# Feed-forward hidden rows: transposed by VectorE in 32x32 squares and sixteen small DMAs, in place of TensorE

## The chip, the cores and the metric

The kernel runs on one core of a Trainium2 chip. TensorE multiplies, VectorE (DVE in the rows) and ScalarE (ACT) do elementwise work, GpSimd (POOL) does a few small steps, and SyncE (SP) issues DMAs. All weights come from the chip's main memory (HBM) in every execution. The metric is the device time of one execution in microseconds (us), the median of several.

## What is computed

Two blocks of two layers each, on 256 tokens of width 1024 in float32. Each layer has two feed-forward stages, a mixer between them and a gated embedding at the end; so there are eight feed-forward stages. Only these are touched:

```python
def swiglu_2(x, wi, wo):
    gate, up = jnp.split(x @ wi, 2, axis=-1)
    return (jax.nn.silu(gate) * up) @ wo

# in every layer, twice (the first block alike, with its own weights):
h = h + 0.5 * rms_norm_2(swiglu_2(rms_norm_2(h, g[0]), ffn_wi_2[i, 0], ffn_wo_2[i, 0]), g[1])
...
h = h + 0.5 * rms_norm_2(swiglu_2(rms_norm_2(h, g[4]), ffn_wi_2[i, 1], ffn_wo_2[i, 1]), g[5])
```

The hidden width is 2816. `x @ wi` gives 2 x 2816 columns, and the product of the gated half with the other half is the left operand of `@ wo`.

## The kernel before, in words

**Matmuls.** A float32 weight is split into a high part (`wh`, written by ScalarE, L634) and a low part (`wl`, the difference, written by VectorE, L820), and so is each left operand (`XH`, `XL`; `AH`, `AL` for the hidden rows). Each product is three matmuls of 128x128 by 128x512: high by high (L516), high by low (L517), low by high (L518).

**Weights.** They come in chunks of mostly 1 MB into three buffers (`raw`), and SP issues the loads in the order of the chunks (`load`, L1109 and L1111: in the up layer of a feed-forward stage two DMAs of 512 KB for a chunk, in the out layer one DMA). A load waits until the chunk three places ahead of it has been split. A chunk has two parts of two rows of tiles each. A part is split into one of seven `wh`/`wl` buffers, so ScalarE rounds part j + 7 (`round`) when TensorE has used part j, and VectorE makes the low part behind it (`leave`). A part is four steps of three matmuls, two steps for each of the two row tiles (t = 0, 1).

**A feed-forward stage.** The up layer has 11 blocks of 512 columns (256 gate columns, 256 up columns), each of 4 parts, so 44 parts in 22 chunks. When both row tiles of block b are done, ScalarE writes tanh of the gate half to a buffer `att` (one of three, L764) and VectorE makes the gated rows of it in four instructions (L966 and L969 for t = 0 and t = 1). These rows have the tokens on the partitions, and the out layer wants them the other way round. So TensorE transposes them, four 128x128 tiles a block, through the identity into a PSUM bank (`pe_turn_hidden`, L542), at a fixed step (12 steps behind the block's last for most blocks; a block has 16). Then ScalarE copies the bank to `AH` (`act_hidden`, L734), and VectorE writes the difference to `AL` (`dve_hidden`, L939). The out layer (22 parts in 12 chunks, two blocks of columns over 22 rows of tiles) reads `AH` and `AL` of hidden block b in its part b.

**Order.** Each engine runs its list in the order in which the code is written: `during` puts extra TensorE work at numbered steps, and the loops over `layer.parts` in `act_ffn`, `dve_ffn`, `act_out` and `dve_out` place the rest at numbered parts. No scheduler moves anything. Engines wait for each other by counting semaphores (`wait_ge`).

Of the kernel before, what the change touches and what calls it, by code (L numbers as in the profile page):

```python
# [14 lines left out]
P = 128  # L15
# [238 lines left out]
class Net:  # L254


    def __init__(self, nc, A, out, ctx, stages):
# [53 lines left out]
        self.AL = at("AL", EO + FF // P * S * 4, [P, FF // P, S], F32R)  # L311

# [113 lines left out]
        self.hid_hi, self.hid_lo = count("hid_hi"), count("hid_lo")  # L426

# [108 lines left out]
    def pe_turn_hidden(self, pe, n, b):  # L536
        bank = self.turn_bank(pe, ("hid", n, b), (self.hid_hi, n, b), (self.hid_lo, n, b))
        hid = self.att[b % 3]
        for i in range(2):
            for t in range(T):  # L540
                pe.wait_ge(self.gated, n, b, t)
                m = pe.e.transpose(bank[:, i * S + t * P:i * S + (t + 1) * P],  # L542
                                   hid[:, t * FB + i * P:t * FB + (i + 1) * P], self.ident[:, :])
        m.then_inc(*self.turned.up("hid", n, b))

# [129 lines left out]
    def act_out(self, act, n):  # L675
# [67 lines left out]
    def act_ffn(self, act, n):  # L743
        layer = self.layers[n, "up"]
        sc = self.cols(2 * T, "sc", n)
        for i, p in enumerate(layer.parts):
# [5 lines left out]
            if i == 7:  # L752
                self.act_hidden(act, n, 0)
            elif i >= 10 and i % 4 == 2:
                self.act_hidden(act, n, i // 4 - 1)
            self.round(act, p.j + N_W)
            if i % 4 == 3:
                b = i // 4
                for t in range(T):
                    act.wait_ge(self.used[t], layer.end[b])  # L760
                    act.wait_ge(self.sc, n, "all")
                    if b >= 3:
                        act.wait_ge(self.turned, "hid", n, b - 3)
                    act.e.activation(self.att[b % 3][:, t * FB:(t + 1) * FB], self.pair((n, "up", b))[t][:, 0:FB],  # L764
                                     ACT.Tanh, scale=sc[:, t:t + 1]).then_inc(*self.tanh.up(n, b, t))
# [129 lines left out]
    def dve_out(self, dve, n):  # L895
# [3 lines left out]
        for i, p in enumerate(layer.parts):  # L899
            if STAGES[n][0] == "ffn" and i == 2:  # L900
                self.dve_hidden(dve, n, NFB - 1)
# [46 lines left out]
    def dve_ffn(self, dve, n):  # L948
        layer = self.layers[n, "up"]
        sc = self.cols(2 * T, "sc", n)  # L950
        for i, p in enumerate(layer.parts):
# [3 lines left out]
            if i == 7:  # L955
                self.dve_hidden(dve, n, 0)
            elif i >= 10 and i % 4 == 2:
                self.dve_hidden(dve, n, i // 4 - 1)
# [12 lines left out]
        self.dve_out(dve, n)
# [140 lines left out]

    def sync(self, e, final):
# [9 lines left out]
        for c in range(self.all_chunks):  # L1123
# [1919 lines left out]
```

## Time and profile before

| | |
|---|---|
| median of 3 runs | 2273.22 us (2271.8 to 2273.25) |
| the profiled execution, its span | 2272.0 us |
| TensorE busy, share of the span | 2238.2 us, 99% |
| VectorE busy | 1467.2 us, 65% |
| ScalarE busy | 1155.1 us, 51% |
| DMA: bytes, mean rate | 395.61 MB, 174 GB/s |
| SP's DMA queue (q1), share of 16 DMA engines | 50.1% |
| granted TensorE clock | 0.998 of full speed, which is 2.4 GHz |

Busy times of matmuls overlap, since one starts before the one ahead of it has ended, so a TensorE at 99% is not at its peak rate. What a step costs is read from the distance between starts, or from the chain of waits: that is the chain of work that ended last, followed back from the end, each piece with the time it adds. Idle time of an engine off that chain costs nothing by itself.

### The profile page before, as it was taken

The page shows a single profiled execution, that of the slowest core. Times are in us where ns is not written, and L with a number is a line of the kernel's source. Part 1 is how long each engine was busy: PE and PEld are TensorE (multiplying, and loading weights), DVE is VectorE, ACT ScalarE, POOL GpSimd, SP SyncE. Part 2 cuts the span into 40 slices and gives each one's busy share as a digit, 9 for nine tenths or more (in the row PEclk, how much of TensorE's full clock was granted, in tenths as well). Part 3 has the DMA queues.
Part 4 walks back from the last instruction along what each step waited for, and adds up shares of the span by engine and source line. Part 5 has one row for each costly group of instructions (what it writes and reads, how often), then busy time and mean ns, then how long its engine had stood idle before and what let it go on. Part 6 is the DMA issues. An engine that isn't in the chain of part 4 may idle for free.

```text
span 2272.0 us, 33788 instructions
## 1 busy us (share of the span) xinstructions
PE 2238.2 (99%) x13383; PEld 1820.8 (80%) x13383; DVE 1467.2 (65%) x2079; ACT 1155.1 (51%) x1668; POOL 180.8 (8%) x286
## 2 busy tenths in 40 slices
PE   8999999999999999999999999999999999999998
PEld 6888888888888768878887888877888788868887
DVE  6655756656765877676567656656656765677655
ACT  5445545445544454354455445455445544565444
POOL 1001001001000010420011001001001100051001
PEclk9999999999999999999999999999999999999999
DMA  7555655555655640065556555534555555526553
GB/s 254 186 185 198 226 177 192 185 186 176 207 188 189 202 160 12 8 222 183 186 179 196 185 186 197 187 94 153 185 188 189 190 185 185 196 76 199 185 177 111
DMA packets 290091, 395.61 MB, mean 174 GB/s; under 512 B 11752, under 2 KB 193328, under 8 KB 289936
## 3 DMA queue, kind: packets, MB, share of 16 engines
q1 hardware_dynamic: 285072, 377.20, 50.1%
q0 software_dynamic: 4720, 16.20, 2.0%
q8 instruction: 108, 1.77, 0.3%
q14 instruction: 47, 0.39, 0.1%
q10 hardware_dynamic: 144, 0.07, 0.0%
HBM read 392.37 MB, written 1.05 MB: 173 GB/s over the span
## 4 chain that ended last, share of the span: by engine, by line
PE 94%; DVE 3%; ACT 1%; issue 1%; POOL 0%; DMA 0%; DVEq 0%; SPq 0%; POOLq 0%; ACTq 0%
PE bank L516 28%; PE bank L518 27%; PE bank L517 27%; PE bank L542 2%; PE bank L530 1%; PE bank L2560 0%; PE bank L1449 0%; PE bank L2554 0%; ACT wh L634 0%; ACT JUNK L641 0%; PE bank L2571 0%; PE bank L1964 0%; PE bank L1186 0%; DVE H L887 0%; DVE qPS L1902 0%
## 5 line engine op out<-in xcount | busy, mean ns | idle before, releaser
L820 DVE TENSOR_TENSOR wl<-raw,wh 128x1024 fp32r<-128x1024 f32 x708 | 859.1, 1223 | 556.5 <-ACT wh L634 556.2
L634 ACT ACTIVATE wh<-raw 128x1024 fp32r<-128x1024 f32 x708 | 744.4, 1058 | 650.9 <-PE bank L518 626.1
L516 PE MATMUL bank<-wh,XH 128*128 128x512 f32 x2000 | 801.7, 401 | 7.0 <-DVE wl L820 5.7
L518 PE MATMUL bank<-wh,XL 128*128 128x512 f32 x2000 | 781.7, 391 | 0.0
L517 PE MATMUL bank<-wl,XH 128*128 128x512 f32 x2000 | 781.5, 391 | 0.0
L516 PEld LDWEIGHTS bank<-wh,XH 128*128 128x128 f32 x2000 | 376.6, 188 | 96.8 <-issue 17.5
L518 PEld LDWEIGHTS bank<-wh,XL 128*128 128x128 f32 x2000 | 376.4, 188 | 81.6
L517 PEld LDWEIGHTS bank<-wl,XH 128*128 128x128 f32 x2000 | 377.2, 189 | 72.6 <-issue 0.5
L516 PE MATMUL bank<-wh,AH 128*128 128x512 f32 x704 | 276.0, 392 | 0.0
L518 PE MATMUL bank<-wh,AL 128*128 128x512 f32 x704 | 274.1, 389 | 0.0
L517 PE MATMUL bank<-wl,AH 128*128 128x512 f32 x704 | 274.1, 389 | 0.0
L518 PEld LDWEIGHTS bank<-wh,AL 128*128 128x128 f32 x704 | 132.2, 188 | 27.5
L517 PEld LDWEIGHTS bank<-wl,AH 128*128 128x128 f32 x704 | 132.2, 188 | 26.8
L516 PEld LDWEIGHTS bank<-wh,AH 128*128 128x128 f32 x704 | 132.2, 188 | 26.9
L1036 POOL TENSOR_SCALAR ST<-ST 128x1 f32<-128x1 f32 x32 | 9.2, 287 | 1358.0 <-ACT JUNK L641 1357.8
L734 ACT ACTIVATE AH<-bank 128x512 fp32r<-128x512 f32 x88 | 52.7, 599 | 113.9 <-PE bank L542 113.9
L939 DVE TENSOR_TENSOR AL<-bank,AH 128x512 fp32r<-128x512 f32 x88 | 60.8, 691 | 57.6 <-ACT AH L734 57.6
L969 DVE SCALAR_TENSOR_TENSOR att<-att,ST,bank 128x256 f32<-128x256 f32 x176 | 84.6, 481 | 6.2
L764 ACT ACTIVATE att<-bank,ST 128x256 f32<-128x256 f32 x176 | 72.3, 462 | 12.7 <-POOL ST L1076 12.7
L966 DVE SCALAR_TENSOR_TENSOR att<-att,bank 128x256 f32<-128x256 f32 x176 | 72.8, 414 | 5.2 <-ACT att L764 5.2
L646 ACT ACTIVATE XH<-CT 128x512 fp32r<-128x512 f32 x60 | 37.2, 628 | 76.6 <-DVE CT L837 71.9
L641 ACT ACTIVATE JUNK<-bank 128x512 bf16<-128x512 f32 x48 | 28.4, 591 | 55.3 <-PE bank L518 55.2
(339 smaller groups left out, 1722.5 us busy)
## 6 DMA issues: line engine op xcount, KB each, us to landing
raw<-in_ffn_w_dram SPq DMA_DIRECT2D x182, 512.0 KB, 4.6
raw<-in_ffn_wi_dram SPq DMA_DIRECT2D x176, 512.0 KB, 4.7
raw<-in_ffn_w_dram SPq DMA_DIRECT2D x40, 1024.0 KB, 4.9
raw<-in_ffn_wo_dram SPq DMA_DIRECT2D x40, 1024.0 KB, 4.8
raw<-in_a_wqkv_dram SPq DMA_DIRECT2D x18, 1024.0 KB, 4.8
raw<-in_a_w_in_dram SPq DMA_DIRECT2D x16, 1024.0 KB, 5.1
raw<-in_b_w_in_dram SPq DMA_DIRECT2D x12, 1024.0 KB, 4.9
bc<-in_norm_g_dram POOLq DMA_DIRECT2D x16, 512.0 KB, 5.2
```

The source lines that it names most:

```text
L516: pe.e.matmul(o, a, h, start=(k == 0), stop=False)
L517: pe.e.matmul(o, a, l, start=False, stop=False)
L518: m = pe.e.matmul(o, b, h, start=False, stop=(k == layer.nk - 1))
L542: m = pe.e.transpose(bank[:, i * S + t * P:i * S + (t + 1) * P], hid[:, t * FB + i * P:t * FB + (i + 1) * P], self.ident[:, :])
L634: act.e.activation(self.wh[j % N_W][:, 0:p.size], self.raw[p.chunk % N_RAW][:, p.at:p.at + p.size], ACT.Copy).then_inc(*self.rounded.up(j))
L646: act.e.activation(self.XH[:, 4 * b:4 * b + 4, t * P:(t + 1) * P], self.CT[b][:, :, :], ACT.Copy).then_inc(*self.x_hi.up(n, t, b))
L734: act.e.activation(self.AH[:, 2 * b:2 * b + 2, :], bank.rearrange("p (k s) -> p k s", k=2), ACT.Copy).then_inc(*self.hid_hi.up(n, b))
L764: act.e.activation(self.att[b % 3][:, t * FB:(t + 1) * FB], self.pair((n, "up", b))[t][:, 0:FB], ACT.Tanh, scale=sc[:, t:t + 1]).then_inc( ...
L820: dve.e.tensor_tensor(self.wl[j % N_W][:, 0:p.size], self.raw[p.chunk % N_RAW][:, p.at:p.at + p.size], self.wh[j % N_W][:, 0:p.size].bitca ...
L939: dve.e.tensor_tensor(lo, bank.rearrange("p (k s) -> p k s", k=2), hi.bitcast(F32), ALU.subtract).then_inc(*self.hid_lo.up(n, b))
L966: dve.e.scalar_tensor_tensor(x, x, 1.0, pair[:, 0:FB], ALU.add, ALU.mult).then_inc(*self.gate.up(n, b, t))
L969: dve.e.scalar_tensor_tensor(x, x, sc[:, T + t:T + t + 1], pair[:, FB:2 * FB], ALU.mult, ALU.mult).then_inc(*self.gated.up(n, b, t))
```

## The change

In each of the eight feed-forward stages, and for each of the 11 hidden blocks:

- `pe_turn_hidden`, its four TensorE transposes and its PSUM bank are gone.
- ScalarE's tanh and VectorE's gating write the `att` buffer with columns in another order (same sizes, the two halves k ahead of the row tiles t), and VectorE transposes the whole buffer in place, 32x32 square by square, right behind the gating (`dve_turn_squares`).
- SP moves the squares to their places in a new float32 tile `AF` with 16 DMAs, each of 32 partitions x 4 runs of 32 floats (128 bytes a run, 16 KB a DMA): eight behind the load of the chunk that is the up layer's chunk 2b + 9, and eight behind the next chunk's load (`sp_hidden`). For b from 7 on these loads belong to the out layer.
- `AF` lies over `AL` (the same bytes); ScalarE copies `AF` to `AH` and VectorE writes `AF` minus `AH` to `AL`. ScalarE waits for the block's 16 DMAs (`d_hid`) where it waited for TensorE.
- Both steps stand later in the order: for block b at part 4b + 12 of the up layer's loop, right behind the tanh (VectorE: the gating) of block b + 2, in place of part 4b + 6 (part 7 for block 0). Blocks 8, 9 and 10 stand at parts 0, 4 and 8 of the out layer's loop, in place of parts 38 and 42 of the up layer's and part 2 of the out layer's.
- ScalarE's tanh of block b + 3 waits for the DMAs of block b, in place of its TensorE transposes.

The diff, cut:

```diff
+        self.AF = at("AF", EO + FF // P * S * 4, [P, FF // P, S], F32)
...
+    def hidden(self, b, t):
+        return self.att[b % 3][:, :].rearrange("p (k t c) -> p k t c", k=2, t=T)[:, :, t, :]
...
-    def pe_turn_hidden(self, pe, n, b):
-        bank = self.turn_bank(pe, ("hid", n, b), (self.hid_hi, n, b), (self.hid_lo, n, b))
...
-            if STAGES[n][0] == "ffn" and i == 2:
-                self.act_hidden(act, n, NFB - 1)
+            if STAGES[n][0] == "ffn" and i in (0, 4, 8):
+                self.act_hidden(act, n, NFB - 3 + i // 4)
...
     def act_hidden(self, act, n, b):
-        bank = self.bank(self.place["turn", ("hid", n, b)])
-        act.wait_ge(self.turned, "hid", n, b)
-        act.e.activation(self.AH[:, 2 * b:2 * b + 2, :], bank.rearrange("p (k s) -> p k s", k=2), ACT.Copy).then_inc(
+        act.wait_ge(self.d_hid[b % 3], n, b, 3, 3)
+        act.e.activation(self.AH[:, 2 * b:2 * b + 2, :], self.AF[:, 2 * b:2 * b + 2, :], ACT.Copy).then_inc(
             *self.hid_hi.up(n, b))
...
-            if i == 7:
-                self.act_hidden(act, n, 0)
-            elif i >= 10 and i % 4 == 2:
-                self.act_hidden(act, n, i // 4 - 1)
+            if i >= 12 and i % 4 == 0:
+                self.act_hidden(act, n, i // 4 - 3)
...
+    def dve_turn_squares(self, dve, n, b):
+
+        hid = self.att[b % 3]
+        dve.wait_ge(self.gated, n, b, 1)
+        dve.e.transpose(hid[:, :], hid[:, :]).then_inc(*self.squares_turned.up(n, b))
...
+    def sp_hidden(self, sp, n, b, half):
+
+        hid = self.att[b % 3][:, :].rearrange("p (k j c) -> p k j c", k=2 * T, j=4)
+        whole = self.AF[:, 2 * b:2 * b + 2, :].rearrange("p k (t i c) -> p (k t) i c", t=T, i=4)
+        sp.wait_ge(self.squares_turned, n, b)
+        for i in (2 * half, 2 * half + 1):
+            for j in range(4):
+                sp.e.dma_start(whole[32 * j:32 * j + 32, :, i, :], hid[32 * i:32 * i + 32, :, j, :]).then_inc(
+                    *self.d_hid[b % 3].up(n, b, i, j, by=16))
...
+            for n in range(self.n_stages):
+                if STAGES[n][0] == "ffn":
+                    block, half = divmod(c - self.layers[n, "up"].parts[0].chunk - 9, 2)
+                    if 0 <= block < NFB:
+                        self.sp_hidden(sp, n, block, half)
```

SP's list in the first up layer, before, where the loads of chunks 9 and 10 stand (`raw` is the weight buffer; a load names the semaphores for which it waits):

```order
L1109 DMA raw_54<-in_ffn_w_dram 128x4x256 [waits left,rounded]
L1111 DMA raw_54<-in_ffn_w_dram 128x4x256
L1109 DMA raw_55<-in_ffn_w_dram 128x4x256 [waits left,rounded]
L1111 DMA raw_55<-in_ffn_w_dram 128x4x256
L1109 DMA raw_56<-in_ffn_w_dram 128x4x256 [waits left,rounded]
L1111 DMA raw_56<-in_ffn_w_dram 128x4x256
```

and the same place now:

```order
L1100 DMA raw_54<-in_ffn_w_dram 128x4x256 [waits left,rounded]
L1102 DMA raw_54<-in_ffn_w_dram 128x4x256
L1111 DMA AF<-att_78 32x4x32 [waits squares_turned]
L1111 DMA AF<-att_78 32x4x32 x7
L1100 DMA raw_55<-in_ffn_w_dram 128x4x256 [waits left,rounded]
L1102 DMA raw_55<-in_ffn_w_dram 128x4x256
L1111 DMA AF<-att_78 32x4x32 x8
```

Behind every load of the stretch stand eight small DMAs, and the next load stands behind them.

VectorE's list at the end of an up block, before (`wl` the low part of a weight, `att` the gated rows):

```order
L820 TENSOR_TENSOR wl_68<-raw_54,wh_61 128x1024 [waits d_raw0,rounded]
L966 SCALAR_TENSOR_TENSOR att_80<-att_80,bank 128x256 [waits tanh]
L969 SCALAR_TENSOR_TENSOR att_80<-att_80,ST,bank 128x256 [waits gate]
L966 SCALAR_TENSOR_TENSOR att_80<-att_80,bank 128x256 [waits tanh]
L969 SCALAR_TENSOR_TENSOR att_80<-att_80,ST,bank 128x256 [waits gate]
L820 TENSOR_TENSOR wl_69<-raw_54,wh_62 128x1024 [waits rounded]
L820 TENSOR_TENSOR wl_70<-raw_55,wh_63 128x1024 [waits d_raw1,rounded]
L939 TENSOR_TENSOR AL<-bank,AH 128x512 [waits hid_hi]
```

and now:

```order
L808 TENSOR_TENSOR wl_68<-raw_54,wh_61 128x1024 [waits d_raw0,rounded]
L956 SCALAR_TENSOR_TENSOR att_80<-att_80,bank 128x2x128 [waits tanh]
L959 SCALAR_TENSOR_TENSOR att_80<-att_80,ST,bank 128x2x128 [waits gate]
L956 SCALAR_TENSOR_TENSOR att_80<-att_80,bank 128x2x128 [waits tanh]
L959 SCALAR_TENSOR_TENSOR att_80<-att_80,ST,bank 128x2x128 [waits gate]
L932 STREAM_TRANSPOSE att_80<-att_80 128x512 [waits gated]
L926 TENSOR_TENSOR AL<-AF,AH 128x512 [waits hid_hi]
L808 TENSOR_TENSOR wl_69<-raw_54,wh_62 128x1024 [waits rounded]
L808 TENSOR_TENSOR wl_70<-raw_55,wh_63 128x1024 [waits d_raw1,rounded]
```

The transpose and the write of `AL` now stand ahead of the low part of the weights for which SP's next load waits.

ScalarE's list at the same place, before:

```order
L764 ACTIVATE att_80<-bank,ST 128x256 [waits used0]
L764 ACTIVATE att_80<-bank,ST 128x256
L634 ACTIVATE wh_62<-raw_54 128x1024 [waits used1]
L634 ACTIVATE wh_63<-raw_55 128x1024 [waits used1,d_raw1]
L734 ACTIVATE AH<-bank 128x512 [waits turned]
```

and now:

```order
L751 ACTIVATE att_80<-bank,ST 128x2x128 [waits used0]
L751 ACTIVATE att_80<-bank,ST 128x2x128
L723 ACTIVATE AH<-AF 128x512 [waits d_hid0]
L624 ACTIVATE wh_62<-raw_54 128x1024 [waits used1]
L624 ACTIVATE wh_63<-raw_55 128x1024 [waits used1,d_raw1]
```

The copy to `AH` now waits for DMAs and stands ahead of the rounding of the next weights.

## Rows read from the trace of the kernel before

**Rows 1.** The page: busy time by engine, and the chain's shares by engine.

```profile
PE 2238.2 (99%) x13383; PEld 1820.8 (80%) x13383; DVE 1467.2 (65%) x2079; ACT 1155.1 (51%) x1668; POOL 180.8 (8%) x286
...
PE 94%; DVE 3%; ACT 1%; issue 1%; POOL 0%; DMA 0%; DVEq 0%; SPq 0%; POOLq 0%; ACTq 0%
```

**Rows 2.** Waits over the span: who for whom, us in total, times, longest.

```profile
ACT wh L634 <- PE bank L518: 626.1, 458, 5.5
...
ACT wh L634 <- DMA raw<-in_ffn_w_dram: 5.9, 5, 2.8
```

**Rows 3.** The chain in order of time, one up block: start us, us, what.

```profile
600.05 0.23 PE bank L518
600.27 0.44 PE bank L542 x4
600.71 0.24 PE bank L516
...
604.17 0.23 PE bank L516
...
611.66 0.44 PE bank L542 x4
```

**Rows 4.** One block's window: us, each engine's busy us, clock, DMA share, GB/s.

```profile
609.49:620.86 11.37, 11.37 (x54) 9.40 (x53) 7.12 (x9) 5.57 (x7) 0.00 (x0) 1.00 0.61 185
```

**Rows 5.** The page's costliest groups: count, busy us, mean ns, idle before.

```profile
L820 DVE TENSOR_TENSOR wl<-raw,wh 128x1024 fp32r<-128x1024 f32 x708 | 859.1, 1223 | 556.5 <-ACT wh L634 556.2
L634 ACT ACTIVATE wh<-raw 128x1024 fp32r<-128x1024 f32 x708 | 744.4, 1058 | 650.9 <-PE bank L518 626.1
...
L734 ACT ACTIVATE AH<-bank 128x512 fp32r<-128x512 f32 x88 | 52.7, 599 | 113.9 <-PE bank L542 113.9
...
L969 DVE SCALAR_TENSOR_TENSOR att<-att,ST,bank 128x256 f32<-128x256 f32 x176 | 84.6, 481 | 6.2
...
L646 ACT ACTIVATE XH<-CT 128x512 fp32r<-128x512 f32 x60 | 37.2, 628 | 76.6 <-DVE CT L837 71.9
```

**Rows 6.** Groups between 300 and 400 us, a VectorE subtraction from SBUF.

```profile
L843 DVE TENSOR_TENSOR XL<-CT,XH 128x512 fp32r<-128x512 f32 x4 | 2.7, 687 | 0.5 <-ACT XH L646 0.4
```

**Rows 7.** ScalarE in time at a block's end: start, us, instruction, idle before.

```profile
605.24 0.82 ACT L764 ACTIVATE att<-bank,ST 128x256 f32<-128x256 f32 x2
606.93 1.06 ACT L634 ACTIVATE wh<-raw 128x1024 fp32r<-128x1024 f32 x1 [0.88 <-PE bank L518]
```

**Rows 8.** VectorE in time at the same block's end.

```profile
607.80 0.48 DVE L969 SCALAR_TENSOR_TENSOR att<-att,ST,bank 128x256 f32<-128x256 f32 x1
608.20 1.22 DVE L820 TENSOR_TENSOR wl<-raw,wh 128x1024 fp32r<-128x1024 f32 x1
```

**Rows 9.** SP's DMA issues in time: start us, us that the issue took.

```profile
1.64 1.98 SPq L1105 DMA_DIRECT2D raw<-in_ffn_w_dram  x4
...
4.73 0.80 SPq L1118 DMA_DIRECT2D H<-in_x_dram  x1
...
609.49 0.37 SPq L1109 DMA_DIRECT2D raw<-in_ffn_w_dram  x1
609.91 0.50 SPq L1111 DMA_DIRECT2D raw<-in_ffn_w_dram  x1
...
756.93 0.96 SPq L2375 DMA_DIRECT2D rW<-in_b_a_dram  x1
```

**Rows 10.** DMA issues over the span: count, KB each, us from issue to landing.

```profile
raw<-in_ffn_w_dram SPq DMA_DIRECT2D x182, 512.0 KB, 4.6
...
out_dram<-H SPq DMA_DIRECT2D x4, 256.0 KB, 2.1
```

**Rows 11.** SP's queue, 600 to 660 us: packets, MB, share of 16 DMA engines.

```profile
q1 hardware_dynamic: 11472, 11.39, 59.5%
```

**Rows 12.** The same, 757 to 760 us, with the sizes of its packets.

```profile
DMA packets 1910, 0.87 MB, mean 290 GB/s; under 512 B 968, under 2 KB 1903, under 8 KB 1910
...
q1 hardware_dynamic: 1910, 0.87, 102.4%
```

More of the change, by code:

```diff
@@ L426, in __init__ @@
         self.hid_hi, self.hid_lo = count("hid_hi"), count("hid_lo")
+        self.squares_turned = count("squares_turned")
+        self.d_hid = [count(f"d_hid{i}") for i in range(3)]
         self.weighed, self.msum, self.rstd, self.resid = (count(x) for x in ("weighed", "msum", "rstd", "resid"))
@@ L534, in x_ready @@
         return lambda k, t: [(self.x_hi, n, t, k // 4), (self.x_lo, n, t, k // 4)]
-    def pe_turn_hidden(self, pe, n, b):
-        bank = self.turn_bank(pe, ("hid", n, b), (self.hid_hi, n, b), (self.hid_lo, n, b))
[L538 to L544, printed above, removed]
     def pe_turn_next(self, pe, n, name, step):
@@ L762, in act_ffn @@
                     if b >= 3:
-                        act.wait_ge(self.turned, "hid", n, b - 3)
-                    act.e.activation(self.att[b % 3][:, t * FB:(t + 1) * FB], self.pair((n, "up", b))[t][:, 0:FB],
+                        act.wait_ge(self.d_hid[b % 3], n, b - 3, 3, 3)
+                    act.e.activation(self.hidden(b, t), self.pair((n, "up", b))[t][:, 0:FB].rearrange(
+                        "p (k c) -> p k c", k=2),
                                      ACT.Tanh, scale=sc[:, t:t + 1]).then_inc(*self.tanh.up(n, b, t))
@@ L899, in dve_out @@
         for i, p in enumerate(layer.parts):
-            if STAGES[n][0] == "ffn" and i == 2:
-                self.dve_hidden(dve, n, NFB - 1)
+            if STAGES[n][0] == "ffn" and i in (0, 4, 8):
+                self.dve_hidden(dve, n, NFB - 3 + i // 4)
             if i == half - 1:
@@ L935, in dve_hidden @@
     def dve_hidden(self, dve, n, b):
-        bank = self.bank(self.place["turn", ("hid", n, b)])
-        hi, lo = (x[:, 2 * b:2 * b + 2, :] for x in (self.AH, self.AL))
+        hi, lo, whole = (x[:, 2 * b:2 * b + 2, :] for x in (self.AH, self.AL, self.AF))
         dve.wait_ge(self.hid_hi, n, b)
-        dve.e.tensor_tensor(lo, bank.rearrange("p (k s) -> p k s", k=2), hi.bitcast(F32), ALU.subtract).then_inc(
-            *self.hid_lo.up(n, b))
+        dve.e.tensor_tensor(lo, whole, hi.bitcast(F32), ALU.subtract).then_inc(*self.hid_lo.up(n, b))
+    def dve_turn_squares(self, dve, n, b):
+        hid = self.att[b % 3]
+        dve.wait_ge(self.gated, n, b, 1)
+        dve.e.transpose(hid[:, :], hid[:, :]).then_inc(*self.squares_turned.up(n, b))
     def dve_p(self, dve, n):
@@ L954, in dve_ffn @@
                 self.dve_p(dve, n)
[L955 to L958, printed above, removed]
+            if i >= 12 and i % 4 == 0:
+                self.dve_hidden(dve, n, i // 4 - 3)
             self.leave(dve, p.j + N_W)
@@ L962, in dve_ffn @@
                 for t in range(T):
-                    x = self.att[b % 3][:, t * FB:(t + 1) * FB]
-                    pair = self.pair((n, "up", b))[t]
+                    x = self.hidden(b, t)
+                    pair = self.pair((n, "up", b))[t].rearrange("p (s k c) -> p s k c", s=2, k=2)
                     dve.wait_ge(self.tanh, n, b, t)
-                    dve.e.scalar_tensor_tensor(x, x, 1.0, pair[:, 0:FB], ALU.add, ALU.mult).then_inc(
+                    dve.e.scalar_tensor_tensor(x, x, 1.0, pair[:, 0], ALU.add, ALU.mult).then_inc(
                         *self.gate.up(n, b, t))
                     dve.wait_ge(self.gate, n, b, t)
-                    dve.e.scalar_tensor_tensor(x, x, sc[:, T + t:T + t + 1], pair[:, FB:2 * FB], ALU.mult,
+                    dve.e.scalar_tensor_tensor(x, x, sc[:, T + t:T + t + 1], pair[:, 1], ALU.mult,
                                                ALU.mult).then_inc(*self.gated.up(n, b, t))
+                self.dve_turn_squares(dve, n, b)
         self.dve_out(dve, n)
```

6 lines of the change are left out of this document (removed).

## The prediction, written before the changed kernel ran

> **What bounds the kernel now.** I read the page first. TensorE is busy 99% of the span and has 94% of the chain that ended last; VectorE is at 65% and ScalarE at 51% [rows 1]. The waits say who follows whom: ScalarE's rounding of weights waits for TensorE 626.1 us in 458 waits, and for a weight DMA 5.9 us in 5 [rows 2]. So the weight pipeline runs ahead, held back by TensorE, and what TensorE no longer does should come off the end. The chain in order of time then prices the transposes [rows 3]: from 600.27 to 611.66 us one block of an up layer passes, 11.39 us. The four transposes are one piece of 0.44 us. From 604.17 to 611.66 stand 33 matmuls, 7.49 us or 0.227 each. From 600.71 to 604.17 stand 15, 3.46 us or 0.231 each: behind the transposes the matmuls are a little slow, 0.06 us in all. In a window of one block VectorE is busy 7.12 us and ScalarE 5.57 of 11.37, the DMA engines 61% [rows 4]. In this stretch there is room everywhere but on TensorE.
>
> **What is removed.** 88 groups of four transposes: the hidden copy to AH has the count, 88 [rows 5]. Each is 0.44 us of the chain, 38.7 us; with all of the slow matmuls behind them it would be 0.50, 44 us. The matmul right behind has 0.24 us for 0.227 [rows 3], so 0.01 at least belongs to the switch: I take 0.45, and 88 x 0.45 = **39.6 us**. A block then takes 10.9 us, a chunk of weights 5.46, a part 2.73.
>
> **What is added on VectorE.** 88 transposes of 128x512 in place. No row shows one. Nearest by size: a VectorE subtraction of 128x512 from SBUF takes 687 ns [rows 6]; the bounds are 481 ns for 128x256 and 1223 ns for 128x1024 [rows 5]. I take 0.69 us. A block costs VectorE 7.12 + 0.69 = 7.8 of 10.9 us, 8.4 at the upper bound. It fits, price nothing as long as the delay doesn't reach TensorE (below). AH is now copied from SBUF, 628 ns by the row of XH, for 599 [rows 5], also hidden. The reordered columns change no size; I price them at nothing.
>
> The Trainium skill ("VectorE: DVE Perf Modes", The three transpose paths) lists TensorE at 390 ns and VectorE at 311 ns for 128x128 in bf16, the latter in 32x32 blocks only. No row here has a VectorE transpose; the sum would be the same by it, since VectorE is not the bound.
>
> **What is added on SP.** 1408 DMAs of 16 KB, eight behind the load of each chunk in 22 of a stage's 34 chunks. SP's own time is the first thing that can run out. Issued alone, a DMA takes 0.37 us, the second of a pair 0.50, and the pair 0.92 from start to end [rows 9]. Four in a row took 1.98 us, 0.50 each [rows 9]. So load and eight small ones are 0.92 + 8 x 0.50 = 4.9 us of a period of 5.46. It fits, but SP goes from idle to 90% full. Bounds per small DMA: 0.37, and 0.96 for one behind others of many short runs [rows 9]; 0.80 was also seen near the start. I take 0.50: these have 128 runs each, fewer than the 256 of the four.
>
> **What is added on the DMA engines.** 1024 packets of 128 bytes a chunk. Between 600 and 660 us a packet (nearly all 1 KB) took 0.595 x 60 x 16 / 11472 = 50 ns [rows 11], so a chunk's load is 1024 x 50 / 16 = 3.2 us of each engine. Between 757 and 760 us, with half of the packets under 512 bytes, the mean was 1.024 x 3 x 16 / 1910 = 26 ns [rows 12]. Bounds for 128 bytes: near zero, and 50. I take 26 as an upper guess: 1024 x 26 / 16 = 1.7 us, 4.9 in all of 5.46. Even at 50 it would be 6.4, and that falls behind by 0.9 us a chunk, 21 us in a stage, about as much as the lead computed below.
>
> **The waits, and the lead.** The second half of block b's DMAs stands behind a load that waits for VectorE's low part; that stands behind VectorE's transpose and AL write, and the AL write waits for ScalarE's AH copy, which waits for the DMAs of the block before. This is a loop, once a block. Before, the low part ran from 608.20 to 609.42 and SP started at 609.49 [rows 8, 9]; now 0.69 + 0.69 us stand ahead of it, so SP starts 1.4 us later. From SP's start: 0.92 + 8 x 0.50 + 2.1 for landing (a small store lands in 2.1, a weight load in 4.6 [rows 10]) = 7.0 us; AH 0.63; rounding 1.06; low part 1.22; hand-offs 0.3: 10.2 us against a block of 10.9. The loop closes in time. In place: a block ends near 604.2, ScalarE comes to the AH copy at 606.06, behind the tanh [rows 7]; the squares have landed at 609.49 - 10.9 + 1.4 + 7.0 = 607.0. So ScalarE waits about 0.9 us a block, and the next rounding, due at 606.93 [rows 7], starts near 607.6. Queued behind that wait are the next weights, and nobody is late: they are for seven parts on, TensorE holds six full ones, 6 x 2.73 = 16.4 us, less the 2.4 us of making one, so a lead of 14 us. In the out layer, block 10 is copied at part 8 and needed at part 10, about 3 us of cover after its 0.63 + 0.69. SP's wait on the squares costs nothing: they are done at 609, and the load that precedes the first half waits for later work. The raw buffers add some 4 us of lead on SP's side: a load is issued about two chunks ahead, 10.9 us, and lands in 4.6, less the 1.4 of the delay. Price of the whole: nothing.
>
> **Sum.** 2272.0 - 39.6 = 2232.4 for the profiled execution; the median lies 1.2 above its span, so **2233.6 us**. Own range, with 0.44 to 0.50 a group: 2229 to 2235.
>
> **Rivals.**
>
> *Stalls at the edges.* The loop keeps time within a stage, but where the up layer ends and where block 10 is needed the lead is short, or the later low part holds the first weights of the next stage. For it: the delay of 1.4 us is on the path by which weights come. Against: only 5.9 us of DMA waits before. At 1 to 3 us a stage, 8 to 24 us of 40 go: 2242 to 2258.
>
> *SP's queue becomes the pace (slower).* Place: SP, up layers. Per chunk SP needs 0.92 + 8x against 5.46. The lag over 22 chunks, less the lead of 14 + 4 = 18 us, reaches TensorE: it decides from x = 0.67 us. At 0.85 (the row of 0.80 and a gap of 0.05): 7.7 us a chunk, 2.26 x 22 - 18 = 31.7 us a stage, 254 in eight, so 2233.6 + 254 = 2487; at 0.96 + 0.04: 8.9 us, 465 us more, near 2700. For it: rows of 0.80 and 0.96. Against: those stood behind DMAs of far more bytes or runs.
>
> *The DMA engines become the pace (slower).* Writes so short may cost more than their bytes. At twice the 50 ns packet: 3.2 + 6.4 = 9.6 us a chunk, (4.1 x 22 - 18) x 8 = 580 us more. It decides from 3.2 + 0.064p = 6.28, p = 48 ns. Against: the 26 ns mean of a mixed stretch. The Trainium skill ("DMA: Bandwidth & Descriptors", Specifications) says that below 512 B the engines read, modify and write, and its rules say to coalesce small transfers; the same page (Why small descriptors are slow) says that moves within SBUF escape the penalty. No row here is a move within SBUF, so both stand.
>
> *No change.* TensorE's list is shorter but something as slow stands behind it, so the 40 us come back as waits: 2269 to 2278. Against: 458 waits of ScalarE for TensorE.
>
> **How the numbers follow.** Chances: hidden 0.64, edges 0.15, no change 0.04, SP 0.10, DMA engines 0.07. The first two are faster by over 0.2% (4.5 us, about what a measurement of this kernel can tell): 0.79; same 0.04; slower 0.17. The range 2227 to 2262 holds the first two, 0.79; its low end leaves 2 us for a larger share of the slow matmuls.
>
> **What would show it.** Right: no L542 in the chain, an up block of 10.9 us, small DMAs issued at 0.50 us or less, ScalarE's AH copy waiting about 1 us for DMAs, rounding still waiting for TensorE. Wrong: matmuls waiting for `wl` or `wh` in the up layers, SP issues of over 0.67 us, a DMA share near 100% there, a weight landing time well over 4.6 us; or AH copies of block 10 that TensorE waits for. A VectorE transpose of over 10.9 - 7.1 = 3.8 us would make VectorE the bound.

## The result, and the profile after

The changed kernel takes 2382.35 us in the median of 4 runs (2379.46 to 2384.24), before 2273.23 us; the ratio is 1.0478, with a 95% interval of 1.0465 to 1.0491. It is 109 us slower, where 40 us faster was foretold.

The page of the changed kernel, first busy time by engine, then the chain that ended last by engine and by line (L1111 is the issue of a square's DMA, L522 to L524 are the three matmuls):

```profile
PE 2242.6 (94%) x13031; PEld 1809.4 (76%) x13031; DVE 1520.8 (64%) x2167; ACT 1129.8 (47%) x1668; POOL 183.6 (8%) x286
...
PE 50%; SPq 26%; DMA 9%; ACT 5%; DVE 4%; issue 4%; POOL 1%; DVEq 0%; POOLq 0%; ACTq 0%
SPq L1111 23%; PE bank L522 14%; PE bank L523 14%; PE bank L524 14%; ACT wh L624 3%; DMA raw<-in_ffn_w_dram 3%; DMA raw<-in_ffn_wi_dram 3%; SPq L1102 2%; SPq L1100 2%; DMA AF<-att 1%; DMA raw<-in_ffn_wo_dram 1%; DVE wl L808 1%; PE bank L536 1%; ACT JUNK L631 1%; PE bank L2566 0%
```

In [rows 1] TensorE had 94% of the chain and SP nothing. Now TensorE has 50% and SP's queue 26%, nearly all of it the squares' issues. SP's issues in time, in an up layer and in an out layer (start us, us, what, how many in a row):

```profile
622.25 0.37 SPq L1100 DMA_DIRECT2D raw<-in_ffn_w_dram  x1
622.67 0.50 SPq L1102 DMA_DIRECT2D raw<-in_ffn_w_dram  x1
623.22 5.10 SPq L1111 DMA_DIRECT2D AF<-att  x8
628.42 0.54 SPq L1100 DMA_DIRECT2D raw<-in_ffn_w_dram  x1
629.01 0.51 SPq L1102 DMA_DIRECT2D raw<-in_ffn_w_dram  x1
629.56 5.10 SPq L1111 DMA_DIRECT2D AF<-att  x8
634.75 0.54 SPq L1100 DMA_DIRECT2D raw<-in_ffn_w_dram  x1
...
1402.89 0.54 SPq L1102 DMA_DIRECT2D raw<-in_ffn_wo_dram  x1
1403.47 5.09 SPq L1111 DMA_DIRECT2D AF<-att  x8
1408.66 0.54 SPq L1102 DMA_DIRECT2D raw<-in_ffn_wo_dram  x1
```

Eight small DMAs take 5.10 us, 0.64 each with the gap between them, and the next load stands right behind: SP has no idle time left. A chunk takes it 634.75 - 628.42 = 6.33 us in the up layer, where TensorE needs a chunk every 5.46, and 5.77 us in the out layer. The page's groups for the copies, the matmuls on AH and VectorE's transpose, and the landing of the small DMAs:

```profile
L522 PE MATMUL bank<-wh,AH 128*128 128x512 f32 x704 | 293.4, 417 | 97.1 <-DVE AL L926 80.0
L723 ACT ACTIVATE AH<-AF 128x512 fp32r<-128x512 f32 x88 | 55.6, 632 | 494.0 <-DMA AF<-att 494.0
...
L926 DVE TENSOR_TENSOR AL<-AF,AH 128x512 fp32r<-128x512 f32 x88 | 60.9, 692 | 312.4 <-ACT AH L723 312.1
...
L932 DVE STREAM_TRANSPOSE att<-att 128x512 f32<-128x512 f32 x88 | 62.6, 712 | 3.0
...
AF<-att SPq DMA_DIRECT2D x1408, 16.0 KB, 2.9
```

ScalarE waits for squares before every one of the 88 copies, 494 us in all or 5.6 us each, where it waited 113.9 us for TensorE [rows 5]. TensorE waits on the hidden rows (97 us at L522, most of it for AL).

Where it waits is plain from the layers. From an up layer's first matmul to the out layer's first, and from there to the out layer's last, the sixth feed-forward stage took 127.6 and 61.0 us before; the changed kernel's takes 123.6 and 78.5. Over the eight stages the out layers went from 60.1 to 61.0 up to 75.7 to 80.1 us, 17 us each, and the up layers got 0.5 to 4.5 us shorter, 26 us in all. 8 x 17 = 136 us, less these 26, is the result.

Two of these stalls, in the fifth stage. ScalarE in time (start us, us, instruction, idle before and what ended it):

```profile
1415.59 0.63 ACT L723 ACTIVATE AH<-AF 128x512 fp32r<-128x512 f32 x1 [6.74 <-DMA AF<-att]
1416.12 1.04 ACT L624 ACTIVATE wh<-raw 128x1024 fp32r<-128x1024 f32 x1
1419.83 2.00 ACT L624 ACTIVATE wh<-raw 128x1024 fp32r<-128x1024 f32 x2 [2.67 <-DMA raw<-in_ffn_wo_dram]
1425.69 1.06 ACT L624 ACTIVATE wh<-raw 128x1024 fp32r<-128x1024 f32 x1 [3.86 <-DMA raw<-in_ffn_wo_dram]
1427.17 0.63 ACT L723 ACTIVATE AH<-AF 128x512 fp32r<-128x512 f32 x1 [0.42 <-DMA AF<-att]
```

VectorE's low parts of blocks 9 and 10:

```profile
1416.25 0.69 DVE L926 TENSOR_TENSOR AL<-AF,AH 128x512 fp32r<-128x512 f32 x1 [5.58 <-ACT AH L723]
...
1427.92 0.68 DVE L926 TENSOR_TENSOR AL<-AF,AH 128x512 fp32r<-128x512 f32 x1
```

TensorE there: the first matmuls of parts 9 and 10, with the idle time before them, and that of part 11:

```profile
1417.09 0.77 PE L522 MATMUL bank<-wh,AH 128*128 128x512 f32 x1 [4.00 <-DVE AL L926]
1428.75 0.77 PE L522 MATMUL bank<-wh,AH 128*128 128x512 f32 x1 [6.35 <-ACT wh L624]
...
1433.24 0.39 PE L522 MATMUL bank<-wh,AH 128*128 128x512 f32 x1
```

and windows of 4 us (busy us and instructions of PE, PEld, DVE, ACT, POOL; granted clock; DMA share; GB/s):

```profile
1408.00:1412.00 4.00, 4.00 (x19) 3.28 (x18) 2.67 (x3) 0.84 (x1) 0.00 (x0) 1.00 0.53 146
1412.00:1416.00 4.00, 1.09 (x5) 0.56 (x3) 0.00 (x0) 0.41 (x1) 0.00 (x0) 0.91 0.36 38
1416.00:1420.00 4.00, 2.91 (x7) 2.36 (x8) 1.92 (x2) 1.33 (x3) 0.00 (x0) 0.50 0.87 280
...
1424.00:1428.00 4.00, 0.00 (x0) 0.00 (x0) 1.22 (x2) 1.88 (x3) 0.00 (x0) 0.69 0.55 131
1428.00:1432.00 4.00, 3.25 (x8) 2.60 (x9) 1.83 (x3) 1.53 (x2) 0.00 (x0) 0.50 1.04 393
```

The hidden rows of blocks 9 and 10 end the two stalls, the second behind weights that had come late too. The view puts the second wait down to a rounding of weights, but `AL` of block 10 was done at 1427.92 + 0.68 = 1428.60 us, and TensorE goes on 0.15 us behind it, as it did behind `AL` of block 9 (1416.94 and 1417.09).

After each of these waits TensorE has the lower clock, 0.50 of full. The first matmul takes 0.77 us for 0.39, and the twelve of part 10 take 1433.24 - 1428.75 = 4.49 us, where those of part 11 take 2.72. The mean granted clock of the span fell from 0.998 to 0.974. The eight out layers are 140 us longer than in the kernel without the DMAs (the first experiment below). 97 of these are the idle time before L522, so the low clock makes up about 43, an estimate by difference. About 18 of the 43 lie behind the last wait of a layer; what lies ahead of a wait only shortens that wait.

### The profile page after: what moved, and what is told of

The parts are those of the page before. It is cut to its first block, busy times and chain, and to the rows that moved or that the text cites. A ratio compares the mean times of both kernels' runs of the same rounds, so it can differ in the third digit from the quotient of the medians.

```text
span 2382.4 us, 34582 instructions
## 1 busy us (share of the span) xinstructions
PE 2242.6 (94%) x13031; PEld 1809.4 (76%) x13031; DVE 1520.8 (64%) x2167; ACT 1129.8 (47%) x1668; POOL 183.6 (8%) x286
## 2 busy tenths in 40 slices
DMA packets 492851, 418.81 MB, mean 176 GB/s; under 512 B 214504, under 2 KB 396080, under 8 KB 492688
## 4 chain that ended last, share of the span: by engine, by line
PE 50%; SPq 26%; DMA 9%; ACT 5%; DVE 4%; issue 4%; POOL 1%; DVEq 0%; POOLq 0%; ACTq 0%
SPq L1111 23%; PE bank L522 14%; PE bank L523 14%; PE bank L524 14%; ACT wh L624 3%; DMA raw<-in_ffn_w_dram 3%; DMA raw<-in_ffn_wi_dram 3%; SPq L1102 2%; SPq L1100 2%; DMA AF<-att 1%; DMA raw<-in_ffn_wo_dram 1%; DVE wl L808 1%; PE bank L536 1%; ACT JUNK L631 1%; PE bank L2566 0%
## 5 line engine op out<-in xcount | busy, mean ns | idle before, releaser
L808 DVE TENSOR_TENSOR wl<-raw,wh 128x1024 fp32r<-128x1024 f32 x708 | 843.7, 1221 | 358.8 <-ACT wh L624 358.3
L624 ACT ACTIVATE wh<-raw 128x1024 fp32r<-128x1024 f32 x708 | 725.3, 1052 | 406.2 <-PE bank L524 267.1
L522 PE MATMUL bank<-wh,XH 128*128 128x512 f32 x2000 | 794.8, 397 | 15.4 <-DVE wl L808 14.1
L524 PE MATMUL bank<-wh,XL 128*128 128x512 f32 x2000 | 781.3, 391 | 0.0
L522 PEld LDWEIGHTS bank<-wh,XH 128*128 128x128 f32 x2000 | 376.9, 188 | 111.1 <-issue 19.0
L524 PEld LDWEIGHTS bank<-wh,XL 128*128 128x128 f32 x2000 | 377.0, 188 | 80.2
L522 PE MATMUL bank<-wh,AH 128*128 128x512 f32 x704 | 293.4, 417 | 97.1 <-DVE AL L926 80.0
L723 ACT ACTIVATE AH<-AF 128x512 fp32r<-128x512 f32 x88 | 55.6, 632 | 494.0 <-DMA AF<-att 494.0
L523 PE MATMUL bank<-wl,AH 128*128 128x512 f32 x704 | 287.7, 409 | 0.0
L524 PE MATMUL bank<-wh,AL 128*128 128x512 f32 x704 | 286.6, 407 | 0.0
L926 DVE TENSOR_TENSOR AL<-AF,AH 128x512 fp32r<-128x512 f32 x88 | 60.9, 692 | 312.4 <-ACT AH L723 312.1
L522 PEld LDWEIGHTS bank<-wh,AH 128*128 128x128 f32 x704 | 140.6, 200 | 139.0 <-issue 93.8
L524 PEld LDWEIGHTS bank<-wh,AL 128*128 128x128 f32 x704 | 140.3, 199 | 31.4
L523 PEld LDWEIGHTS bank<-wl,AH 128*128 128x128 f32 x704 | 141.2, 201 | 28.8
L932 DVE STREAM_TRANSPOSE att<-att 128x512 f32<-128x512 f32 x88 | 62.6, 712 | 3.0
```

What stands on the lines that cost most here:

```text
L522: pe.e.matmul(o, a, h, start=(k == 0), stop=False)
L523: pe.e.matmul(o, a, l, start=False, stop=False)
L524: m = pe.e.matmul(o, b, h, start=False, stop=(k == layer.nk - 1))
L624: act.e.activation(self.wh[j % N_W][:, 0:p.size], self.raw[p.chunk % N_RAW][:, p.at:p.at + p.size], ACT.Copy).then_inc(*self.rounded.up(j))
L723: act.e.activation(self.AH[:, 2 * b:2 * b + 2, :], self.AF[:, 2 * b:2 * b + 2, :], ACT.Copy).then_inc(*self.hid_hi.up(n, b))
L808: dve.e.tensor_tensor(self.wl[j % N_W][:, 0:p.size], self.raw[p.chunk % N_RAW][:, p.at:p.at + p.size], self.wh[j % N_W][:, 0:p.size].bitca ...
```

## The experiments

Where one execution is named, the kernel was timed once. The kernel before took 2270.7 to 2276.2 us beside all of these runs.

**Without the DMAs.** ScalarE and VectorE read `att` itself:

```diff
-        act.wait_ge(self.d_hid[b % 3], n, b, 3, 3)
+        act.wait_ge(self.squares_turned, n, b)
...
-                        self.sp_hidden(sp, n, block, half)
```

> Left out: the sixteen DMAs. ScalarE and VectorE take AH and AL straight from the att buffer behind VectorE's transpose, so the hidden rows stand in the wrong places. Theory A (SP's issuing is the pace; VectorE's and TensorE's side of the change is as foretold): the whole gain shows, an up block of 10.9 us, 2228 to 2234 us. Theory B (the later places of the copies, or VectorE's transpose ahead of the weights' low part, cost the time): still well above 2273.

Measured: 2230.18 us in one execution, span 2228.4. The chain in order of time, in an up layer (start us, us, what):

```profile
599.95 0.23 PE bank L522
600.18 0.23 PE bank L523
600.41 0.23 PE bank L524
...
611.51 0.23 PE bank L522
```

From 599.95 to 611.51 stand 51 matmuls, 0.227 us each, with nothing between them. So the gain was there, 2272.3 to 2228.4 us for the spans, 44 us, or 0.50 a group: the upper end of the foretold price. VectorE's transpose and the later copies cost nothing. All of the loss is in the sixteen DMAs.

**Fewer DMAs for the same bytes.** Eight a block, runs of 256 bytes:

```diff
-            for j in range(4):
-                sp.e.dma_start(whole[32 * j:32 * j + 32, :, i, :], hid[32 * i:32 * i + 32, :, j, :]).then_inc(
+            for j in range(2):
+                q = 32 * ((i + 1) % 4)
+                sp.e.dma_start(whole[q:q + 32, :, 2 * j:2 * j + 2, :], hid[32 * i:32 * i + 32, :, 2 * j:2 * j + 2, :]).then_inc(
```

> Eight DMAs a block in place of sixteen, four behind a load, with the same bytes in all (32 partitions x 4 runs of 256 bytes; squares land in the wrong places). Theory A (SP's time): 1.1 + 4 x 0.64 = 3.7 us a chunk against 5.46, so SP has time to spare and the kernel takes 2230 to 2240 us. Theory D (the bytes, or the latency of a move behind a load, is the pace and not the number of issues): little better than 2382.

Measured: 2238.14 us in one execution. SP's issues there:

```profile
610.52 0.37 SPq L1100 DMA_DIRECT2D raw<-in_ffn_w_dram  x1
610.94 0.51 SPq L1102 DMA_DIRECT2D raw<-in_ffn_w_dram  x1
611.49 2.53 SPq L1112 DMA_DIRECT2D AF<-att  x4
614.48 0.37 SPq L1100 DMA_DIRECT2D raw<-in_ffn_w_dram  x1
```

The issues cost the same 0.64 us each, but now SP waits for the pipeline again, and the 144 us are gone. All eight feed-forward stages are as long as without the DMAs, to 0.5 us. The 8 us above that kernel lie in the mixer, where TensorE ran at clock 0.50 from 865 to 882 us in this execution and at 1.00 in the other. Theory A stands against theory D: the bytes are the same. The packets are half as many too, though; the next kernels keep the number of issues and change the rest.

**What makes an issue cost 0.64 us.** Three kernels change the DMA alone: 32 runs of 512 bytes; all 128 partitions without a shift; and a source in HBM.

```diff
+                sp.e.dma_start(whole[q:q + 32, j, :, :], hid[32 * i:32 * i + 32, j, :, :]).then_inc(
...
+                sp.e.dma_start(whole[:, j, i, :], hid[:, i, j, :]).then_inc(
...
+                sp.e.dma_start(whole[32 * j:32 * j + 32, :, i, :], self.A["c_ident"][32 * i:32 * i + 32, :].rearrange(
```

> Sixteen DMAs a block of the same 16 KB each, as 32 runs of 512 bytes in place of 128 runs of 128; squares land in the wrong places. Theory A1 (an issue costs SP 0.64 us whatever its runs): eight in a row still 5.1 us, 2382 us. Theory A2 (the issue's price grows with the number of runs): eight in a row under 4.2 us and 2235 to 2260 us. Theory C (the DMA engines are held up by 128-byte packets): packets a quarter, so the time falls as in A2, but the issues on SP stay at 0.64 us.

> Sixteen DMAs a block, each over all 128 partitions with one run of 128 bytes, no shift between partitions (squares land in the wrong places); bytes, runs and DMA count as in the changed kernel. Theory A1 (fixed price of an issue): eight in a row 5.1 us, 2382 us. Theory A3 (the price comes from 32 partitions x 4 runs, two levels of pattern): eight in a row about 4.0 us, the 0.50 of the weight loads, and 2233 to 2245 us.

> The sixteen DMAs of the changed kernel with the same shape and place, but read from HBM (a constant) in place of the squares, so the hidden rows are wrong. Tells what made an issue 0.64 us where four weight loads in a row took 0.50. Theory S (a source in SBUF makes the issue dear): eight in a row 4.0 us, 2235 to 2260 us. Theory R (any DMA in a long row of DMAs costs it): eight in a row 5.1 us, 2375 to 2390 us.

Measured, one execution each: 2358.69, 2369.87 and 2379.55 us. Eight in a row, in this order:

```profile
704.09 4.94 SPq L1112 DMA_DIRECT2D AF<-att  x8
```
```profile
703.02 5.02 SPq L1111 DMA_DIRECT2D AF<-att  x8
```
```profile
703.95 5.05 SPq L1111 DMA_DIRECT2D AF<-in_c_ident_dram  x8
```

It is 4.9 to 5.1 us whatever the runs, the partitions or the source; the first kernel has a quarter of the packets, and 128 us of its time above 2230 remain. So the price is one of an issue as such when many stand in a row, and the number of packets isn't the cause. The small differences fit as well: summed over the trace, the 1408 issues take 863.0 us in the changed kernel and 838.9, 850.8 and 860.5 in these three, which is 24.1, 12.2 and 2.5 less, and the medians are 23.7, 12.5 and 2.8 us less. Why four weight loads at the start of the kernel took 0.50 each [rows 9] and these take 0.64 stays open.

**Off SP.** Half of the squares, then all, through GpSimd's queue, behind `pool_gain`:

```diff
+        pool.wait_ge(self.squares_turned, n, b)
+        for i in range(4):
+            for j in js:
+                pool.e.dma_start(whole[32 * j:32 * j + 32, :, i, :], hid[32 * i:32 * i + 32, :, j, :]).then_inc(
+                    *self.d_hidp[b % 3].up(n, b, i, j, by=16))
```

> Squares of column groups 2 and 3 are moved by GpSimd's queue, eight DMAs a block, as soon as VectorE has turned them; groups 0 and 1 by SP, four behind a load. Theory A (SP's time is the pace): SP 1.1 + 4 x 0.64 = 3.7 of 5.46 us, GpSimd 8 x 0.6 = 4.8 of 10.9: 2230 to 2240 us, faster than both kernels. Theory D (bytes or packets on the DMA engines): 2380.

> All sixteen DMAs from GpSimd's queue behind the turning, none from SP. GpSimd's issues took 0.53 to 0.62 us before, 16 of them 8.5 to 9.9 of 10.9 us, landed about 17 us behind the block's end and asked for at 23.7. Theory A: 2230 to 2240 us. Rival: with short runs a GpSimd issue costs over 0.68 us, and then it is the pace in place of SP; at 0.8 it lags 1.9 us a block and the kernel is between 2240 and 2400.

Measured: half 2240.39 us (2230.86 to 2241.26), ratio to before 0.9844 (0.9823 to 0.9865); all 2232.84 us (2231.87 to 2239.3), ratio 0.983 (0.9812 to 0.9847). GpSimd's issues, one row of the second kernel's:

```profile
629.83 8.67 POOL L1124 DMA_DIRECT2D AF<-att  x16 [2.23 <-DVE att L933]
```

Sixteen take it 8.67 us of a block's 10.9, 0.54 each, and then it waits for the next squares. The same 1408 DMAs with the same bytes cost nothing when they don't stand ahead of the weight loads. By themselves these two runs don't clear the DMA engines. In the trace SP's squares are packets of 128 bytes, 180224 of them in the changed kernel, and GpSimd's are packets of 1 KB. So the second kernel has no packet of 128 bytes, and the first has half as many. The next kernel has all 180224 again.

**Fewer issues by way of HBM.** Four DMAs write a block's squares to a scratch in the layout of AF, one reads it back a chunk later:

```diff
+        if half == 0:
+            sp.wait_ge(self.squares_turned, n, b)
+            for i in range(4):
+                sp.e.dma_start(dr.rearrange("(j c) (k i p) -> i c k j p", j=4, k=4, i=4)[i], hid[32 * i:32 * i + 32, :, :, :]).then_inc(
+                    *self.d_square[b % 3].up(n, b, i, by=16))
+            return
+        sp.wait_ge(self.d_square[b % 3], n, b, 3)
+        sp.e.dma_start(self.AF[:, 2 * b:2 * b + 2, :], dr.rearrange("q (k s) -> q k s", k=2)).then_inc(
+            *self.d_hid[b % 3].up(n, b, by=16))
```

> The squares go through a scratch in HBM: four DMAs (32 partitions x 16 runs of 128 bytes) write them behind the first load, one DMA of 128 partitions x 2 KB reads them back behind the next. Five issues a block in place of sixteen. Theory A: SP 0.92 + 4 x 0.64 = 3.5 us and 0.92 + 0.5 = 1.4 us a chunk: never the pace; 2230 to 2240 us. Rival: the runs of 128 bytes cost more on their way to HBM, or the wait for the write (over 3 us) holds up the weight loads behind it on SP: 2245 to 2300.

Measured: 2228.55 us (2226.72 to 2237.71), ratio to before 0.981 (0.9788 to 0.9831): 1.9% less than the kernel before, and as fast as the kernel without the DMAs. SP and the waits for these rows:

```profile
1261.70 4.30 SPq L1113 DMA_DIRECT2D hid_squares<-att  x4
1267.67 0.37 SPq L1102 DMA_DIRECT2D raw<-in_ffn_wi_dram  x1
1268.08 0.51 SPq L1104 DMA_DIRECT2D raw<-in_ffn_wi_dram  x1
1268.63 0.50 SPq L1117 DMA_DIRECT2D AF<-hid_squares  x1
```
```profile
ACT AH L725 <- DMA AF<-hid_squares: 27.7, 24, 2.9
```

The writes are dearer than foretold: these four took 0.58, 1.45, 0.72 and 1.43 us, and the 88 rows of four 2.6 to 6.5 us, 4.2 in the median; but a block is 10.9 us long. ScalarE waits 27.7 us in all for them. The packets of the second GpSimd kernel and of this one:

```profile
DMA packets 335155, 418.81 MB, mean 188 GB/s; under 512 B 34280, under 2 KB 238384, under 8 KB 334992
```
```profile
DMA packets 488620, 441.76 MB, mean 199 GB/s; under 512 B 199016, under 2 KB 380592, under 8 KB 488464
```

The changed kernel has 214504 packets under 512 bytes. This one has nearly as many, more bytes, and loses nothing, and that rules out the DMA engines as the cause. They have little room left, though: from 600 to 660 us their share is 0.87, where it was 0.60 before.

**Which work the lag reaches TensorE by.** The first try left block 10 to TensorE, at its old step:

```diff
+            if step == 12:
+                self.pe_turn_hidden(pe, n, NFB - 1)
...
-                    if 0 <= block < NFB:
+                    if 0 <= block < NFB - 1:
```

> Block 10 of each stage goes over TensorE as before (copy still at part 8 of the out layer); blocks 0 to 9 as in the changed kernel. Theory A (SP falls behind by some 0.87 us a chunk and the lag comes out at the hidden block that the out layer needs first): SP has two of 22 slots less, 11.6 us, but block 9 is then the late one and is needed one part, 2.7 us, sooner: of the 17 us that an out layer is longer 8 to 10 stay, about 2310 us. Theory E (only block 10 is short of cover, the others aren't): the out layer is as short as before, about 2240 us.

Measured: 2353.2 us in one execution, above both. The out layers are 71.7 to 75.2 us. TensorE's waits (us in total, times, longest):

```profile
PE bank L547 <- DVE att L976: 46.5, 16, 7.1
PE bank L522 <- DVE AL L943: 26.5, 8, 4.4
```

Its transposes (L547) now wait for gated rows: ScalarE's tanh of block 10 was late. So not only the copies were late but ScalarE's whole list. I hadn't foreseen this wait.

**SP's lag with nobody waiting for the squares.** To the kernel without DMAs I added as many from a constant into scratch, at the same places in SP's list, in four of the eight stages:

```diff
+        sp.wait_ge(self.squares_turned, n, b)
+        for i in (2 * half, 2 * half + 1):
+            for j in range(4):
+                sp.e.dma_start(row[32 * j:32 * j + 32, :, i, :], self.ident[32 * i:32 * i + 32, :].rearrange(
+                    "p (k c) -> p k c", k=4)).then_inc(*self.d_hid[b % 3].up(n, b, i, j, by=16))
```

> The kernel without DMAs of squares (hidden rows taken straight from att, in the wrong places), plus SP's sixteen DMAs a block as fillers (identity into scratch), at the same places in SP's list, in the four second feed-forward stages alone. Nobody but the weight loads waits behind them. Theory G (the weights' lead of some 18 us takes up SP's lag of 17 to 21 us; the loss came from the hidden rows, which have about 4 us of cover): 2230 to 2245 us. Theory H (late weight loads alone make the loss, as much as in the changed kernel, 17 us a stage): 2230 + 4 x 17 = 2298 us.

Measured: 2312.48 us in one execution, 82 us over 2230. 75 of them lie in the four out layers with fillers, 17 to 21 each; the rest lies in the mixer behind the third stage. Theory G falls: late weight loads alone are enough. But its profile has the same place. In the second feed-forward stage TensorE, then ScalarE:

```profile
511.21 0.77 PE L523 MATMUL bank<-wh,AH 128*128 128x512 f32 x1 [16.56 <-DVE AL L927]
```
```profile
494.80 1.06 ACT L625 ACTIVATE wh<-raw 128x1024 fp32r<-128x1024 f32 x1 [4.63 <-DMA raw<-in_ffn_w_dram]
501.79 2.00 ACT L625 ACTIVATE wh<-raw 128x1024 fp32r<-128x1024 f32 x2 [5.94 <-DMA raw<-in_ffn_w_dram]
508.15 1.06 ACT L625 ACTIVATE wh<-raw 128x1024 fp32r<-128x1024 f32 x1 [4.36 <-DMA raw<-in_ffn_w_dram]
509.12 0.61 ACT L724 ACTIVATE AH<-att 128x512 fp32r<-128x512 f32 x1
```

TensorE waits 16.56 us for AL of block 10. The rows for it had long been in `att`; ScalarE's copy stood behind four roundings of weights that TensorE needs only several parts later, and these waited for late loads.

**The same, with the copies ahead.**

```diff
-            if STAGES[n][0] == "ffn" and i in (0, 4, 8):
-                self.act_hidden(act, n, NFB - 3 + i // 4)
+            if STAGES[n][0] == "ffn" and i < 3:
+                self.act_hidden(act, n, NFB - 3 + i)
```

> As the fillers kernel, but the AH and AL copies of blocks 8, 9 and 10 stand at parts 0, 1 and 2 of the out layer's loop on ScalarE and VectorE, in place of 0, 4 and 8; SP's list is the same. The fillers kernel lost 20 us in each of four stages with no squares to wait for. Theory J (ScalarE's list is in order, the copy of block 10 stood behind the rounding of weights that come off SP late, and it is needed two parts later; the weights themselves are needed seven parts later): with the copies ahead, the loss falls from 20 to under 5 us a stage, 2230 to 2250 us. Theory H (late weights reach TensorE by themselves): 2300 to 2315 us, as before the move.

Measured: 2268.93 us in one execution, 39 us over 2230, 9 to 11 a stage. The order of three copies was worth half of the loss. The other half is more than theory J had: here TensorE waits for weights (24.4 us for `wl` in 9 waits), so each theory holds for a part. This split is shown for the fillers alone. In the changed kernel the squares of block 10 are themselves issued behind SP's late loads, and no run tells how much of its loss comes by each way.

**How many slots it takes.** Blocks 0 to 4, then 0 to 7, by DMAs, the rest by TensorE; and the five-block kernel with ScalarE's and VectorE's copies four parts later:

```diff
+            if step >= 44 and (step - 44) % 16 == 0 and (step - 44) // 16 + 1 >= NDMA:
+                self.pe_turn_hidden(pe, n, (step - 44) // 16 + 1)
...
-                    if 0 <= block < NFB:
+                    if 0 <= block < NDMA:
```

> Blocks 0 to 4 of each stage go by squares and DMAs, blocks 5 to 10 by TensorE at their old steps (copies at the new parts). Theory A with a lead (SP falls behind by at most 10 slots x 0.87 = 9 us, less than the 14 us by which the weights run ahead, and catches up): no stall, 40 groups x 0.49 = 19.6 us less than before, 2253 us. Rival F (every slot costs TensorE its 0.87 us at once): 2253 + 10 x 0.87 x 8 = 2323 us.

> Blocks 0 to 7 by squares and DMAs, 8 to 10 by TensorE. Theory A with a lead: 16 slots, a lag of 13 to 14 us, just what the lead holds: 64 groups x 0.49 = 31 us less, 2242 us, or up to 5 us a stage more if block 10's transposes wait for rows that ScalarE has late: 2242 to 2282. Rival F: 2242 + 16 x 0.87 x 8 = 2353 us.

> As the kernel with five blocks by DMAs, but ScalarE and VectorE take these five blocks four parts later (part 4b + 16), so they don't wait for squares. The five-block kernel was 38 us over the 2253 foretold. Theory K (ScalarE's waits for squares made its tanh late, and TensorE's transposes of the later blocks waited for the gated rows): no such waits, 2253 to 2262 us. Theory L (SP's late weight loads make ScalarE late in any case): 2275 to 2292 us.

Measured, one execution each: 2291.96, 2309.51 and 2296.46 us. All out layers of the first kernel take 60.1 to 61.0 us, as before; the loss is in the up layers, where two stalls a stage, of 0.4 to 1.1 and of 1.6 to 3.1 us, stand at TensorE's transposes of blocks 6 and 7. Neither side of my expectation holds: there is some lead, since the five-block kernel is 31 us under rival F, but far from 14 us of it. The later copies bring nothing back, so ScalarE's waits for squares are not the cause. With them gone it waits 216 us for weight loads, where it waited 44 in the first kernel and 6 before. That speaks for theory L, late weights, though the time lies above its range too. These mixed kernels have a wait of their own, since a copy at part 4b + 12 holds the PSUM bank that TensorE needs for block b + 2, so their sizes say little about the changed kernel.

## Why the prediction was wrong, point by point

- **Removed: right in kind, a little small.** 0.50 us a group where I took 0.45 (the kernel without DMAs). The slow matmuls behind the transposes went with them.
- **VectorE: right.** 0.712 us for 0.69 foretold, hidden. AH from SBUF 0.632 for 0.628.
- **SP, the first step that failed.** I took 0.50 us an issue from one row of four at the start of the kernel [rows 9] and reasoned that fewer runs could only be cheaper. It is 0.64, and three other shapes and sources are as dear. The pair of loads between such rows took 1.14 us and not 0.92. So load and squares took SP 6.33 us and not 4.9, over the 5.46 that it had. The prediction had SP at 90% full; a sum 23% too low turns the answer round there.
- **The lead, the second.** With 0.64 my own rival still said no loss, since it put the point from which SP decides at 0.67; with the measured 6.33 us it says 0.87 x 22 - 18 = 1 us a stage. The lag itself was about what its formula gives, 19 us: in the fifth stage, from the load of the up layer's tenth chunk to that of the out layer's ninth, SP takes 110 us in the kernel without DMAs and 132 in the changed one, a lag of 22 us. TensorE is 4 us later at the end of that up layer and 13 more at part 10 of the out layer, where it needs block 10. So the lead was about 5 us and not 18. I had taken the lead of the weights, seven parts, for that of ScalarE. Its list is in order, and between the roundings stands work of short cover: the copy of block 10, needed two parts later. When a load is late, this waits with it. I had even priced that cover at 3 us, and then compared the lag with the other number. The fillers show it without any squares (17 to 21 us a stage), and the moved copies bring back half of it. In the changed kernel the squares of block 10 are late as well, by SP's own lag.
- **The loop and ScalarE's waits.** Foretold 0.9 us a block, measured 5.6 (494 in 88). A small DMA landed in 2.9 us where I took 2.1. Once SP is the pace, every wait behind it grows.
- **Clock.** Not in the sum. The two stalls shown are followed by matmuls at half clock (0.77 us for 0.39 at 1417.09 and at 1428.75 us), and over the out layers this comes to about 43 of the 140 us.
- **DMA engines: right.** Not the pace: the trip through HBM moved as many packets of 128 bytes and lost nothing. Such a packet took 13 ns in the mean of the changed kernel's trace, so the 26 from a mixed stretch [rows 12] was twice too high, on the safe side. Of the two statements of the Trainium skill that the prediction set side by side, the runs go with the one that moves within SBUF are not slowed (DMA: Bandwidth & Descriptors, Why small descriptors are slow). With 90112 packets of 128 bytes within SBUF, on a queue of SP with room left, the first GpSimd kernel took 2231 to 2241 us, and a packet of 128 bytes took 13 ns beside 27 for one of 512 (the kernel with runs of 512 bytes).
- **Stall at the edges.** The place was right, the out layer's block 10, but it came from SP's lag and not from the 1.4 us.

The same page of the Trainium skill (DMA: Bandwidth & Descriptors, Issuing engines are not separate DMA queues) says that spreading DMAs over issuing engines saves only their issue time, and that is usually small. In this case the issue time was all of the loss: 2382 us from SP, 2233 from GpSimd.

## What to carry to other kernels

Count the issues on a DMA queue as work of an engine, with a duration from a long row of them, and compare the sum with the period in which the loads behind them must go out; at 90% full, look for fewer or another queue before moving work there. When a lag meets a lead, take the shortest cover (the time between a result's due place in the list and its first use) of anything in the late engine's list, not the cover of the work that is late. And where a move between partitions needs many small DMAs, a trip through HBM can need a third of them; here it took the DMA engines to a share of 0.87.

## What was not expected of the hardware

An issue from SP costs 0.60 us and a gap of 0.04 when several small DMAs stand in a row, with 32 or 128 runs, 32 or 128 partitions, from SBUF or HBM; the first two loads after a pause cost 0.37 and 0.50. GpSimd's cost 0.54. Four DMAs of 64 KB in runs of 128 bytes to HBM took 2.6 to 6.5 us to issue, 4.2 in the median. The same 16 KB moved in packets of 128 bytes when SP issued the DMA and of 1 KB when GpSimd did. After waits of 4.00 and 6.35 us TensorE ran at 0.50 of its clock. In the kernel before it did so only near the start of the first stage (mean 0.58 from 22 to 26 us); from 35 to 2265 us the mean is 1.00.
